# Eight query units of a fused decoder block moved from three-pass fp32r to plain fp32, with gathered rows taken among them

## The reference, cut to what is computed

```python
z = h @ w_in[l]                       # q | k | v | conv B, C, h | two gates
attn = sliding_window_sink_attention(q, k, v, sinks[l]) @ w_attn_out[l]
conv = (cb * causal_short_conv(cc * ch, conv_w[l])) @ w_conv_out[l]
merged = gates[..., :D_MODEL] * attn + gates[..., D_MODEL:] * conv
h = layer_norm(ALPHA * h + merged @ w_o[l], ln1_g[l], ln1_b[l])      # LN1
# PEER: 8 heads, two sets of 128 sub-keys each
q = (xt @ w_q).reshape(t_, PEER_HEADS, 2, PEER_HALF)                 # query units
s = jnp.einsum('thpc,hpnc->thpn', q, sub_keys)                       # key scores
top_s, top_i = lax.top_k(s, PEER_TOPK)      # 16 of each set, then 16 of the sums
u = jnp.take(u_tab, ec, axis=0)             # 128 experts a token
act = gelu(jnp.einsum('cd,chkd->chk', xc, u)); wgt = gate * act
y = jnp.einsum('chk,chkd->cd', wgt, jnp.take(v_tab, ec, axis=0))
h = layer_norm(ALPHA * h + y, ln2_g[l], ln2_b[l])
```

## Time and profile before

| | |
|---|---|
| median of three runs | 3862.97 us (3860.53 to 3867.95) |
| profiled execution, device time | 3854.19 us |
| profiled execution, first to last instruction | 3852.4 us |
| busy: PE, DVE, ACT, POOL | 3753.8, 2716.0, 1384.7, 1140.0 us |
| chain that ended last, by engine | PE 84%, DMA 8%, DVE 6% |
| mean DMA rate over the span | 321 GB/s |

### The profile page before, as it was taken

One profiled execution on the slowest core, in us unless ns is written; L12 is line 12 of the kernel. 1 busy time (PEld: TensorE's weight loads), 2 busy tenths in 40 slices (PEclk: granted clock), 3 DMA queues, 4 the chain that ended last, 5 costly groups with the idle time before them and its releaser, 6 DMA issues.

```text
span 3852.4 us, 60802 instructions
## 1 busy us (share of the span) xinstructions
PE 3753.8 (97%) x24487; PEld 3474.4 (90%) x24487; DVE 2716.0 (71%) x3363; ACT 1384.7 (36%) x1969; POOL 1140.0 (30%) x595
## 2 busy tenths in 40 slices
PE   8999999999999999999999999999999899999997
PEld 8999999999988888888888899999999877878886
DVE  4544555456688755656555588888888788888988
ACT  5544444444423100000000344566663334444443
POOL 0000000000734443534443473233233334233431
PEclk9999999999999999999999999999999999999999
DMA  5344554554589999999999559999999999999996
GB/s 189 110 153 178 184 185 181 181 184 175 220 360 385 403 422 403 402 397 404 392 409 376 208 183 395 381 393 386 379 381 422 402 399 402 391 375 393 402 393 245
DMA packets 193198, 1234.84 MB, mean 321 GB/s; under 512 B 20160, under 2 KB 37136, under 8 KB 49936
## 3 DMA queue, kind: packets, MB, share of 16 engines
q1 hardware_dynamic: 107792, 657.56, 44.4%
q0 software_dynamic: 73728, 536.90, 34.2%
q10 hardware_dynamic: 11520, 38.28, 2.5%
HBM read 1194.39 MB, written 37.75 MB: 320 GB/s over the span
## 4 chain that ended last, share of the span: by engine, by line
PE 84%; DMA 8%; DVE 6%; issue 1%; ACT 1%; SPq 0%; ACTq 0%; DVEq 0%
PE dense_ps L941 22%; PE dense_ps L930 13%; PE dense_ps L932 13%; PE dense_ps L931 13%; PE dense_ps L1181 7%; DMA wbuf<-in_w_units_dram 4%; PE score_ps L1181 3%; PE dense_ps L973 3%; DMA wbuf<-in_peer_v_dram 3%; PE oT_ps L1181 2%; PE o_ps L1181 2%; DMA row<-in_peer_v_dram,expert 2%; PE o_ps L1066 1%; DVE h L1238 1%; PE score_ps L1138 1%
## 5 line engine op out<-in xcount | busy, mean ns | idle before, releaser
L1284 DVE TENSOR_TENSOR w_lo<-wbuf,w_hi_r 128x1024 fp32r<-128x1024 f32 x800 | 972.7, 1222 | 552.9 <-ACT w_hi_r L581 551.6
L581 ACT ACTIVATE w_hi_r<-wbuf 128x1024 fp32r<-128x1024 f32 x872 | 917.5, 1059 | 1158.4 <-PE dense_ps L932 555.8
L930 PE MATMUL dense_ps<-act_hi,w_hi_r 128*128 128x256 f32 x4128 | 1181.4, 286 | 26.4 <-DVE w_lo L1284 25.8
L931 PE MATMUL dense_ps<-act_lo,w_hi_r 128*128 128x256 f32 x4128 | 1171.4, 284 | 0.0
L932 PE MATMUL dense_ps<-act_hi,w_lo 128*128 128x256 f32 x4128 | 1171.3, 284 | 0.0
L930 PEld LDWEIGHTS dense_ps<-act_hi,w_hi_r 128*128 128x128 f32 x4128 | 795.7, 193 | 35.9 <-DVE w_lo L1284 26.4
L931 PEld LDWEIGHTS dense_ps<-act_lo,w_hi_r 128*128 128x128 f32 x4128 | 795.8, 193 | 0.0
L932 PEld LDWEIGHTS dense_ps<-act_hi,w_lo 128*128 128x128 f32 x4128 | 795.3, 193 | 0.0
L941 PE MATMUL dense_ps<-xT,wbuf 128*128 128x256 f32 x3136 | 686.4, 380 | 0.8 <-ACT xT L566 0.8
L941 PEld LDWEIGHTS dense_ps<-xT,wbuf 128*128 128x128 f32 x3136 | 593.1, 190 | 85.6 <-issue 5.3
L532 POOL DMA_INDIRECT row<-in_peer_v_dram,expert x199 | 417.7, 2099 | 805.4 <-DVE h L1238 780.5
(11 more groups left out here) (241 smaller groups left out, 4328.5 us busy)
## 6 DMA issues: line engine op xcount, KB each, us to landing
wbuf<-in_w_units_dram SPq DMA_DIRECT2D x456, 1024.0 KB, 6.6
wbuf<-in_peer_v_dram SPq DMA_DIRECT2D x128, 1024.0 KB, 9.2
act_spill<-stage ACTq DMA_DIRECT2D x64, 256.0 KB, 8.9
gate_spill<-gbuf ACTq DMA_DIRECT2D x8, 2048.0 KB, 10.5
e_act<-act_spill SPq DMA_DIRECT2D x32, 512.0 KB, 9.7
e_gate<-gate_spill SPq DMA_DIRECT2D x32, 512.0 KB, 11.6
row<-in_peer_u_dram,expert POOLq DMA_INDIRECT x256, 13.7
row<-in_peer_v_dram,expert POOLq DMA_INDIRECT x199, 11.1
```

Of the source, the lines that this page charges most:

```text
L581: act.activation(w_hi[:, j, :], wbuf[n % 2][:, j, :], ACT.Copy).then_inc(w_hi_ready, 1)
L930: nc.tensor.matmul(out, w[0], x[0], start=opens, stop=False)
L931: nc.tensor.matmul(out, w[0], x[1], start=False, stop=False)
L1284: V.tensor_tensor(w_lo[n % 2][:, j, :], wbuf[n % 2][:, j, :], w_hi[:, j, :].bitcast(F32), ALU.subtract).then_inc(lo_by_dve, 1)
```

## The change

The second half's query units (156 to 163) become plain. The transposed `h` then goes whole into `aT`, with no low part; the vectors of LN1, which lie in `aT`, are laid out by quarters so that a quarter of them is free when the transposes of its columns come. The scores, which lay in `aT` too, go through a ring of four in `kT`, with a wait of ACT for the selection four units back, and the row slot over `kT` (9) is not used before the selection is done. The slots 3 to 6, over `w_hi` and `act_lo`, stay in use up to row 270 instead of 258. DVE takes 16 rows among the query units (5, 2, 2, 2, 0, 2, 2, 1), so that by unit 228 only 86 rows are left for the last 62 units, and not 102. The split of the activations for unit 164 is a step of its own: ACT writes `act_hi` at the fifth and sixth unit, DVE `act_lo` ahead of `pick(5)` and `pick(6)`. POOL makes the low parts of 164 to 167 only; ahead of `low(164)` in its queue stand all gathers up to row 274.

```diff
@@ -76,12 +76,12 @@
-    return UNITS <= n < UNITS + U_PQ
+    return UNITS <= n < N_U
...
-    return U_PQ < n < UNITS or UNITS + U_PQ < n < N_U + 4
+    return U_PQ < n < UNITS or N_U <= n < N_U + 4
@@ -107,15 +107,15 @@
         return 2 if r == U_OUT else 4 if r % 4 == 0 else 3
-    return 1 if r == U_PQ - 2 else 0
+    return (1, 0, 5, 2, 2, 2, 0, 2, 2, 1)[r - (U_PQ - 2)]
...
-EARLY_ROWS, LATE_ROWS = ROWS_TO[UNITS + U_PQ - 3], ROWS_TO[N_V + 1]
-PHASES = ((0, (0, 1, 2, 3, 4, 5, 6)), (EARLY_ROWS, (0, 1, 2, 9)), (LATE_ROWS, (0, 1, 2, 7, 9)))
+EARLY_ROWS, MIDDLE_ROWS, LATE_ROWS = ROWS_TO[UNITS + U_PQ + 4], ROWS_TO[N_U + 2], ROWS_TO[N_V + 1]
+PHASES = ((0, (0, 1, 2, 3, 4, 5, 6)), (EARLY_ROWS, (0, 1, 2)), (MIDDLE_ROWS, (0, 1, 2, 9)), (LATE_ROWS, (0, 1, 2, 7, 9)))
 SLOT, USE, FREE = {}, {}, {}
@@ -200,6 +200,7 @@
                 for k, at_ in enumerate((w_hi_at, ln2_at, xT_at)) for i in range(2)]
+        ks_ring = over(kT_at, "ks_ring", [P, 4, TILES, 2, NK], F32)
         row.append(over(kT_at, "row_kv", [P, D], F32))
@@ -238,6 +239,7 @@
         ks = aT[:, :, :].rearrange("p k t -> p (k t)").rearrange("p (c t a k) -> p c t a k", c=PH, t=TILES, a=2)
+        ks_at = lambda b, c: ks_ring[:, c % 4, :, :, :] if b else ks[:, c, :, :, :]
         onehot = scratch(0, 2048).rearrange("p (s k) -> p s k", k=TOPK)
@@ -254,7 +256,7 @@
         subk = mflat[:, 0:2048].rearrange("p (g c) -> p g c", g=2 * PH)
-        ln1 = aT[:, :, :].rearrange("p k t -> p (k t)").rearrange("p (a d) -> p a d", a=2)
+        ln1 = aT[:, :, :].rearrange("p k t -> p (k t)").rearrange("p (c a d) -> p c a d", c=4, a=2)
         h1 = cT[:, :, :].rearrange("p k t -> p (k t)").rearrange("p (t d) -> p t d", t=TILES)
@@ -299,6 +301,8 @@
         tr_lo = sem("tr_lo")
+        h_hi = sem("h_hi")
+        h_lo = sem("h_lo")
         m_hi = sem("m_hi")
@@ -429,8 +433,8 @@
                 sp.wait_ge(dense_ready, n0 + U_OUT)
-                sp.dma_start(ln1[:, 0, :], ln1_g[0, :].partition_broadcast(P)).then_inc(ln1_in, 16)
-                sp.dma_start(ln1[:, 1, :], ln1_b[0, :].partition_broadcast(P)).then_inc(ln1_in, 16)
+                sp.dma_start(ln1[:, :, 0, :], ln1_g[0, :].partition_broadcast(P).rearrange("p (c d) -> p c d", c=4)).then_inc(ln1_in, 16)
+                sp.dma_start(ln1[:, :, 1, :], ln1_b[0, :].partition_broadcast(P).rearrange("p (c d) -> p c d", c=4)).then_inc(ln1_in, 16)
                 for n in range(n0 + U_PQ, n0 + UNITS):
@@ -529,6 +533,8 @@
                 pool.wait_ge(row_used, FREE[g] + START)
+                if SLOT[g] == 9 and USE[g] == 1:
+                    pool.wait_ge(pick_step, 4 * 2 * PH + START)
                 pool.indirect_dma_start(
@@ -539,13 +545,13 @@
             pool.wait_ge(dense_ready, UNITS)
-            for g in range(3, ROWS_TO[UNITS + U_PQ - 2] + 4):
+            for g in range(3, ROWS_TO[N_U - 3] + 3):
                 gather(g)
-            for n in range(UNITS + U_PQ + 1, N_U + 4):
+            for n in range(N_U, N_U + 4):
                 low(n)
-                for g in range(ROWS_TO[n - 3] + 4, ROWS_TO[n - 2] + 4):
+                for g in range(ROWS_TO[n - 3] + 3, ROWS_TO[n - 2] + 3):
                     gather(g)
-            for g in range(ROWS_TO[N_U + 1] + 4, LATE_ROWS):
+            for g in range(ROWS_TO[N_U + 1] + 3, LATE_ROWS):
                 gather(g)
@@ -563,14 +569,14 @@
                     act.wait_ge(tr_ready, 8 * call + r + 1)
-                    act.activation((xT if call == 2 else act_hi)[:, 2 * r:2 * r + 2, :].rearrange("p k t -> p (k t)"),
+                    act.activation((xT if call == 2 else aT if call == 3 else act_hi)[:, 2 * r:2 * r + 2, :].rearrange("p k t -> p (k t)"),
                                    tr_ps(call, r)[:, :, :].rearrange("p k t -> p (k t)"), ACT.Copy).then_inc(tr_done, 1)
...
                     return
-                if n == UNITS + U_PQ and j == 0:
+                if n == N_U and j == 0:
                     act.wait_ge(row_used, EARLY_ROWS + START)
@@ -751,6 +757,9 @@
+                def split_h_hi(r):
+                    act.activation(act_hi[:, 2 * r:2 * r + 2, :], aT[:, 2 * r:2 * r + 2, :], ACT.Copy).then_inc(h_hi, 1)
                 def gate_units(base, group, bias, i, first=False, last=False):
@@ -827,9 +836,13 @@
                         move_transposes(2, 0, 2)
+                    if b and c in (4, 5):
+                        for r in range(4 * (c - 4), 4 * (c - 3)):
+                            split_h_hi(r)
                     act.wait_ge(ks_ready, at_ + 1)
-                    act.activation(ks[:, c, :, :, :].rearrange("p t a k -> p (t a k)"),
+                    if b and c >= 4:
+                        act.wait_ge(pick_step, 4 * (at_ - 4) + 2 + START)
+                    act.activation(ks_at(b, c).rearrange("p t a k -> p (t a k)"),
                                    score_ps[c % 2][:, :, :].rearrange("p t k -> p (t k)"), ACT.Copy).then_inc(ks_out, 1)
@@ -901,6 +914,8 @@
                         pe.wait_ge(tr_done, 16 + r - 2)
+                    elif call == 3 and r >= 5:
+                        pe.wait_ge(tr_done, 24 + r - 4)
                     elif call != 2 and r >= 5:
@@ -935,15 +950,15 @@
                     j = 2 * c + k // 8
-                    if plain(n):
-                        if k == 0:
-                            pe.wait_ge(w_ready[2 * (n % 2) + c], (8 * per) * i + 16 * (n // 2 + 1))
-                        last = nc.tensor.matmul(dense_ps[n % 4][:, c, :], w_part(wbuf[n % 2], n, k, j), src[:, k, :],
-                                                start=opens and k == 0, stop=closes and k == KT - 1)
+                    if plain(n) and k == 0:
+                        pe.wait_ge(w_ready[2 * (n % 2) + c], (8 * per) * i + 16 * (n // 2 + 1))
                     if k % 8 == 0 and not plain(n):
...
                     if split_at is not None and k % 2 == 0:
-                        pe.wait_ge(tr_lo, split_at + k // 2 + 1)
+                        pe.wait_ge(split_at[0], split_at[1] + k // 2 + 1)
+                    if plain(n):
+                        last = nc.tensor.matmul(dense_ps[n % 4][:, c, :], w_part(wbuf[n % 2], n, k, j), src[:, k, :],
+                                                start=opens and k == 0, stop=closes and k == KT - 1)
                     if not plain(n):
@@ -1114,14 +1129,15 @@
                 n = n0 + U_PQ
-                acts = (act_hi, act_lo)
+                acts = aT if b else (act_hi, act_lo)
+                moved = (tr_done, 24) if b else (tr_lo, 8)
                 pe.wait_ge(dense_out, n)
...
                 begin(n, 0, 0)
-                half_T(n, acts, 0, k1=8, split_at=8 * b + 8)
+                half_T(n, acts, 0, k1=8, split_at=moved)
                 half_T(n, acts, 1, k1=8, used=0, opens=False)
                 transposes(2 * b + 1, hs[b], 4)
-                half_T(n, acts, 0, k0=8, used=2, closes=False, split_at=8 * b + 8)
+                half_T(n, acts, 0, k0=8, used=2, closes=False, split_at=moved)
                 half_T(n, acts, 1, k0=8)
@@ -1139,8 +1155,9 @@
+            acts = (act_hi, act_lo)
             begin(N_U, 0, 0)
-            half_T(N_U, acts, 0)
+            half_T(N_U, acts, 0, split_at=(h_lo, 0))
             query_scores(1, 7)
@@ -1504,13 +1521,13 @@
                         V.scalar_tensor_tensor(out=hs[b][:, t, part_c], in0=hs[b][:, t, part_c], scalar=mv[:, t, 0:1],
-                                               in1=ln1[:, 0, part_c], op0=ALU.subtract, op1=ALU.mult
+                                               in1=ln1[:, c, 0, :], op0=ALU.subtract, op1=ALU.mult
                                                ).then_inc(ln_step, 1)
...
                         V.scalar_tensor_tensor(out=hs[b][:, t, part_c], in0=hs[b][:, t, part_c], scalar=rstd[:, t:t + 1],
-                                               in1=ln1[:, 1, part_c], op0=ALU.mult, op1=ALU.add).then_inc(h_ready, 1)
-                    if c % 2:
+                                               in1=ln1[:, c, 1, :], op0=ALU.mult, op1=ALU.add).then_inc(h_ready, 1)
+                    if c % 2 and not b:
                         split_transposes(2 * b + 1, 4 * (c // 2), 4 * (c // 2) + 4)
@@ -1520,12 +1537,13 @@
                     d = c - 1
+                    ksc = ks_at(b, c) if first else None
                     if first:
...
                         for t, a in both:
-                            last = V.max(tops[c % 2][a][:, t, 0:8], ks[:, c, t, a, :])
+                            last = V.max(tops[c % 2][a][:, t, 0:8], ksc[:, t, a, :])
                         last.then_inc(pick_step, 1)
@@ -1544,9 +1562,9 @@
                         for t, a in both:
-                            V.max_index(at_k(t, a, 0), tops[c % 2][a][:, t, 0:8], ks[:, c, t, a, :])
+                            V.max_index(at_k(t, a, 0), tops[c % 2][a][:, t, 0:8], ksc[:, t, a, :])
                         for t, a in both:
```

(15 more changed lines are left out.)

## The result

The changed kernel takes 3893.3 us (median of four runs, 3889.5 to 3896.8) against 3863.6: a ratio of 1.0078, 95% interval 1.0066 to 1.0090. It is slower by 30 us; 3878, slower by 15, was forecast, with 3893.0 as the upper end.

The account below looks back on a forecast made before the run. PE was taken to pace the kernel, with transfers a second limit after 2900 us. Pace +18.3, wait +8, clock +2 and relief -13 summed to +15.3 us, put on the median of 3863.0: 3878 us, range 3860 to 3893.

Parts of the forecast that it names:

- Pace: Query units 156 to 163: each plain unit takes 2.29 us longer on PE, +18.3 us for eight.
- a count of four passes: Plain query units: four passes at 3.84 us give 15.4 us a unit, 31 us for eight; the trace shows 13.81.
- Relief of the V units: Units from 228 on: 86 rows instead of 102 cut PE's waits and clock loss, -13 us, bounds 0 and 25.
- The wait at unit 164: Start of unit 164: PE waits for POOL's low part behind a gather released by DVE's row, +8 us.
- The start of unit 165: First low part there at 2305 us, PE finishing unit 164 at 2304.6: called "Even", no wait added.
- The clock's share: Around the wait at unit 164: the clock falls while PE waits, 1.3 to 5 us lost, taken as +2 us.
- the DMA share: Sign for the V units: share under 0.95 after the change, with PE's waits there down from 12 to about 2.
- the signs of being wrong: Wrong if DVE reaches row 271 before PE ends 163, V waits stay, or U-unit waits move.
- may give back 1.5: First operation of find_keys(0) took 1.68 us beside POOL; with POOL quiet there, 1.5 us might be regained.
- Slower, DVE's delay is passed on: Rival: late selection delays unit 168 or the gate's exp, PE loses 10 us more; +25, 3888 us, chance 0.08.
- The rows removed pay nothing: Rival: V waits come from DVE's and ACT's order, not bytes, so only costs stay; +28, 3891 us, chance 0.11.
- The late stretch pays back all: Rival: waits after 2900 us share one transfer backlog that 16 rows tip; -22, 3841 us, chance 0.11.

Follow-up runs that it names:

- f4: Changed kernel with POOL writing zeros by memset instead of subtracting for the low parts of units 164 to 167; units 163 to 168 took 66.4 us.
- e4: Kernel before with seven rows among its query units, which stay three-pass, leaving 95 rows for the last 62 units; ratio 1.0065.
- f3: Kernel before with the last 16 of the 512 rows left out, neither gathered nor added; ratio 0.9970.
- g1: Changed kernel with seventeen early rows (8, 5, 2, 2), splits together, fewer gathers ahead, two rows instead of three in each of units 212 to 227; ratio 0.9941.
- g3: Kernel before with two and three rows in turn in units 212 to 227, so 110 rows in the last 62 units; ratio 0.9969.
- g4: Kernel before with two rows instead of three in each of units 212 to 227, so 118 rows for the last 62 units; ratio 0.9946.
- e3: Changed kernel with POOL's gathers two rows less ahead, so the low parts of 164 and 165 stand only behind gathers with free slots; ratio 1.0046.

## Why the prediction was wrong

- *Pace.* Right: +18.3 forecast, +17.7 measured, the copies of the units (2289.24 - 2186.30)/7 = 14.71 us apart, as forecast. Plain fp32 cost what the plain stretch had shown. The prediction says that the trace disagrees with a count of four passes. It disagrees only with the price of 3.84 us a pass, which is that of fp32r. A plain unit is 32 matmuls of 256 columns, and 13.81/32/4 = 0.108 us, an estimate of 259 cycles at 2.4 GHz (the granted clock is 1.00 there); an fp32r matmul of the same size takes 0.120 us, 288 cycles. So the time fits four passes of about a column a cycle each, and it is the fp32r pass that is dearer.
- *Relief of the V units.* Right: -13 forecast, -12.0 in the changed kernel, -9 to -11 when the rows were simply left out. PE's waits there fell from 19.4 to 10.7 us, of which 8.3 are the one long wait that the forecast left in place. How near the sizes are is in part chance: five executions with 86 rows took 737.3 to 741.6 us in this stretch, three with 102 rows 750.7 to 762.5. One sign failed: from 3156 to 3800 us the DMA share was 0.97, not under 0.95. And the prediction's "no stretch here shows more than 413" overlooks the page, where two slices have 422 GB/s.
- *The wait at unit 164.* Right in place, mechanism and near in size: 6.9 us and not 8, right behind the gathers of rows 273 and 274, which DVE's two rows after `pick(5)` released.
- *The start of unit 165.* This step failed. I followed both queues to "Even", with 12.4 + 2 us for PE and durations of DVE from rows where POOL was quiet. POOL's first four subtractions held DVE's splits for 9.4 us, `pick(6)` began that much later, and the same chain (row, gather, low part) ran late again: 8.9 us of wait, and 1.2 in unit 166. The clock's share grew with the waits: less its waits the stretch is 5.8 us longer than before (22.7 - 16.9), where +2 was forecast for one wait; in f4, with one long wait, it is 2.0 (7.9 - 5.9). The granted clock from 2293 to 2320 us was 0.75. Forecast for 163-168: 58.5 + 10 = 68.5 us; measured 81.2. f4, which takes the contention away, gives 66.4, or some 69 with the 3 us of POOL's shorter operations put back, close to the forecast; so this one missing term accounts for the error, 12.7 of the 14.4 us. It was in none of the signs of being wrong either: DVE did not reach row 271 too early, the V waits fell, and those of the U units stayed (22.8 and 20.8 us).
- *The sign was in the trace.* The earlier trace rows has the operation of 128x128 that took 1.68 us beside POOL, and I wrote that POOL's quiet "may give back 1.5". I read contention as something the change takes away from `find_keys(0)`, and didn't ask what in the new order falls beside POOL's work. The Trainium skill (GPSIMD Engine Reference, 1. Specifications) says that GpSimd's path to SBUF is shared with VectorE, which contends with it when its instruction has two SBUF inputs or is in a 2-port mode. The runs agree, with the numbers above: rows and splits, which have two inputs in SBUF, are held, and the selection's own instructions are not (`pick(7)`, from 2315.5 to 2322.8 us, took its usual 7.4 us although POOL subtracted from 2317.69 on). The shift that took 10.45 us in e4 reads one tensor only; whether it ran in a 2-port mode no run here shows.
- *"Slower, DVE's delay is passed on", 3888 us with 0.08,* came near in size, by luck: DVE's delay was passed on, but not where this case put it. PE had no wait at unit 168, and 168-179 took 127.4 us as before. The range ended at 3893.0, and the contention was in none of its bounds.
- *"The rows removed pay nothing"* would have given 3891 and looks as if it had come true. f3 and the last stretch rule it out: two errors of opposite sign would be needed.
- *"The late stretch pays back all"* is wrong for this change, but its premise, that 211-227 is where rows hurt, is what g1, g3 and g4 turned into a gain: I had put those 22.8 us aside as not touched by the change.

## What to carry to other kernels

When work is moved to an engine's idle time, look at what the engine beside it does in those very microseconds: durations from rows where the neighbour was quiet are lower bounds. And a queue that waits for the held engine passes the hold on and adds its own. Before paying for a new place for some work (here 17.7 us of PE time for 16 rows), look at how the plan spreads it over places that are full already; moving 16 rows from the fullest 16 units to the 62 after them gave 20 us net.

## What the runs showed of the hardware

- A DVE instruction with two operands in SBUF that meets a run of POOL subtractions, each begun as the one before ends, was mostly held until the run ended, and not for one instruction: it ended 0.6 us (split) and 2.2 us (row, about its own duration) after POOL's last of four. A DVE operation of 0.2 us with one operand took 10.45 beside a run of seven. There are two exceptions. The operation of 1.68 us in the earlier trace rows ended at 2242.66 us, 0.1 us after the first of two subtractions, although the second began at 2242.55; the high part that this second one needs was ready at 2242.48 only. And in e3 (below) a row ended while a subtraction ran. Who begins first does not settle it: the split of 10.19 us had begun 0.3 us before POOL. What decides stays open.
- A memset of POOL did not hold the one split that met it in f4 (0.68 us as elsewhere, begun 0.3 us before the memset, as the split of 10.19 us was before a subtraction). The rows there, 2.33 us, met no memset, so f4 does not show what a memset does to a row.
- The hold goes both ways. In e3 DVE was first, by 0.17 us: two POOL subtractions took 8.78 us and not 4.8 while DVE worked on rows (6.75 us for two, not 4.8), and the two engines took turns:

```profile
2286.17 6.75 DVE L1255 SCALAR_TENSOR_TENSOR h<-row,dots,h 128x2048 f32<-128x2048 f32 x2
...
2286.34 8.78 POOL L527 TENSOR_TENSOR w_lo<-wbuf,w_hi_r 128x1024 fp32r<-128x1024 f32 x2 [2.00 <-ACT w_hi_r L587]
```

- Transfers at 1.00 of their engines' time and 410 GB/s left PE without a gap in g4, at 1.01 and 413 GB/s they cost it 23 of 201 us: a full queue says nothing on whether it is behind. What made the difference was one row a unit, and a unit's bytes over the rate, beside PE's own time, tell it.
